# A two-layer encoder on one core: modulation columns by 32x32 transposes on VectorE, and GpSimd's branch ahead of its index wait

## What is computed

```python
for l in range(DEPTH):
    mod = ca @ w_ada[l] + b_ada[l]                    # (1, 6 * 1024)
    sh1, sc1, gt1, sh2, sc2, gt2 = split(mod, 6)
    h = rms_norm(x, g_norm1[l]) * (1.0 + sc1) + sh1
    proj = h @ w_in[l]                                # groups A, B, C, D
    ...
    mix = concat([ya, yb, yc, yd]) @ w_out[l]
    x = x + gt1 * mix
    h2 = rms_norm(x, g_norm2[l]) * (1.0 + sc2) + sh2
    x = x + gt2 * hier_moe(h2, ...)                   # 32 experts, top 2
return rms_norm(x, g_final)
```

## Time and profile before

| | us |
|---|---|
| three runs | 2034.39, 2034.10, 2145.37 |
| median | 2034.39 |
| the profiled execution | 2032.44 |
| its span, first to last instruction | 2030.6 |
| PE busy in it | 1684.3 (83%) |
| DVE busy | 581.1 (29%) |
| ACT busy | 509.1 (25%) |
| POOL busy | 225.0 (11%) |
| mean granted clock of TensorE | 0.896 |

### The profile page before, as it was taken

How to read it: one execution, slowest core, us unless ns; L and a number is a source line. 1 busy time by engine, 2 the same in 40 slices (tenths; PEclk the granted TensorE clock), 3 DMA queues, 4 the chain that set the end, 5 groups by cost and what they waited for, 6 DMA issues and landing times. The chain is left out here.

```text
span 2030.6 us, 22742 instructions
## 1 busy us (share of the span) xinstructions
PE 1684.3 (83%) x7696; PEld 843.4 (42%) x7696; DVE 581.1 (29%) x1259; ACT 509.1 (25%) x1109; POOL 225.0 (11%) x223
## 2 busy tenths in 40 slices
PE   4999987998878988788849999889688788888882
PEld 3456544455333333333325655444534333333331
DVE  1373344233111111111146515432311111112114
ACT  2101745322111111112131026461111111112112
POOL 2000012010111011111130002021101111111101
PEclk7999967988999989899969998689699899999896
DMA  9423433126999889999971324320378999999993
GB/s 337 148 83 124 143 124 102 52 116 261 409 399 402 338 336 398 396 399 418 375 243 62 105 95 151 125 102 21 124 294 353 394 403 402 403 416 401 389 406 138
DMA packets 91445, 527.49 MB, mean 260 GB/s; under 512 B 13936, under 2 KB 20176, under 8 KB 66800
## 3 DMA queue, kind: packets, MB, share of 16 engines
q1 hardware_dynamic: 72720, 489.43, 61.2%
q0 software_dynamic: 13104, 24.51, 3.9%
q10 hardware_dynamic: 5552, 12.65, 1.7%
HBM read 521.04 MB, written 23.86 MB: 268 GB/s over the span
## 5 line engine op out<-in xcount | busy, mean ns | idle before, releaser
L1090 PE MATMUL ps<-ring,arena 128*64 128x512 f32 x2928 | 703.5, 639 | 160.0 <-DMA ring<-in_w_exp_up 140.9
L1090 PEld LDWEIGHTS ps<-ring,arena 128*64 128x64 f32 x2928 | 254.6, 147 | 565.6 <-issue 562.0
L822 PE MATMUL ps<-ring,hT 128*128 128x512 f32 (+1 forms) x1024 | 363.7, 513 | 6.5 <-ACT tmp L1260 4.9
L822 PEld LDWEIGHTS ps<-ring,hT 128*128 128x128 f32 x1024 | 192.4, 190 | 164.2 <-issue 147.3
L576 DVE TENSOR_TENSOR arena<-ps,arena 64x512 f32<-64x512 f32 (+1 forms) x64 | 44.4, 693 | 688.3 <-ACT arena L1359 443.3
L1359 ACT ACTIVATE arena<-ps 128x512 f32<-128x512 f32 x64 | 38.2, 597 | 618.5 <-PE ps L1090 586.1
L782 POOL DMA_INDIRECT yexp_d<-arena,masks x64 | 59.3, 927 | 927.0 <-DVE arena L584 927.0
L1351 ACT ACTIVATE arena<-ps,modc 128x128 f32<-128x128 f32 x256 | 96.4, 457 | 51.7 <-PE ps L1078 51.0
L565 DVE TENSOR_SCALAR arena<-ps,modc 128x128 f32<-128x128 f32 x256 | 87.4, 403 | 44.3 <-PE ps L1078 42.4
L1078 PEld LDWEIGHTS ps<-cst,arena 128*128 128x128 f32 x512 | 64.6, 195 | 66.3 <-issue 66.1
L1511 DVE SCALAR_TENSOR_TENSOR probsT<-z,convw,probsT 128x512 f32<-128x512 f32 x120 | 89.9, 751 | 3.6
(11 more groups left out here) (182 smaller groups left out, 1351.3 us busy)
## 6 DMA issues: line engine op xcount, KB each, us to landing
ring<-in_w_exp_gate SPq DMA_DIRECT2D x64, 2048.0 KB, 14.7
ring<-in_w_exp_up SPq DMA_DIRECT2D x64, 2048.0 KB
ring<-in_w_exp_down SPq DMA_DIRECT2D x64, 2048.0 KB, 10.0
ring<-in_w_ada SPq DMA_DIRECT2D x24, 2048.0 KB, 9.4
ring<-in_w_in SPq DMA_DIRECT2D x8, 2048.0 KB, 19.4
ring<-in_w_out SPq DMA_DIRECT2D x4, 2048.0 KB
ring<-in_w_in SPq DMA_DIRECT2D x6, 1024.0 KB, 16.8
xn_d<-arena ACTq DMA_DIRECT2D x8, 512.0 KB, 2.6
```

The costliest lines, as they stand in the source:

```text
L822: last = pe.matmul(out, lhs(k), rhs(k), start=(k == 0), stop=(k == n - 1))
L1090: last = [pe.matmul(outs[c][HALF * c:HALF * c + HALF, :], lhs(k)[:, 0:HALF], rhs(c, k), start=(k == 0), stop=(k == n - 1), tile_position=( ...
```

## The change

Ten column units are done in another way: units 6 to 9 of both layers, in the attention loop, and units 2 and 3 of layer 1, behind the lists (`turned_columns`). The first six of the program and all gates stay as they are. For a turned unit ACT makes no copy. DVE transposes the bank in blocks of 32x32 to `tmp` (`ada_turned`, two instructions of 128x256), so that the 32 equal rows of a group become 32 equal columns. `mod` then takes one column of each block and makes two products, with a stationary 128x32 table `fold32` of four stacked identities, which adds the four groups up, and eight moving columns. Apart from that, POOL's wait for the index list moves from ahead of the branch into both of its arms.

```diff
@@ CONSTS
-          "cosA": TT * DIFF, ...
+          "fold32": 32, "cosA": TT * DIFF, ...
@@ program
+        def turned_columns(l, u):
+            return u // 2 % 3 != 2 and (u >= NORM1_UNITS or (l and u >= NORM1_UNITS // 2))
@@ route (DVE)
             for m, u in ADA_NEXT[l][:2]:
                 mod_out(m, u)
+            for n, (m, u) in enumerate(ADA_NEXT[l][2:]):
+                ada_turned(m, u, n)
             link(slot_lists((l, "more_lists"), NE, P))
@@ gpsimd
                 words = wide_words(pool, l)
-                pool.wait_ge(gidx_ready, l + 1)
                 def gather(e):
                     def body(w):
+                        if e == 0:
+                            pool.wait_ge(gidx_ready, l + 1)
                         if e >= 2:
@@ mod (PE)
                 p0 = HALF * (u % 2)
+                if turned_columns(l, u):
+                    picked = tmp[:, part, :].rearrange("p (h k r) -> p h k r", h=2, k=KD)
+                    for h in range(2):
+                        q0 = p0 + 32 * h
+                        last = pe.matmul(bank(key)[q0:q0 + 32, 0:KD], C["fold32"], picked[:, h, :, 0],
+                                         start=True, stop=True, tile_position=(0, q0))
+                    fills(last, key)
+                    return
                 for k in range(KD):
@@ scalar, attention loop
                         m, u = ADA_LATER[l][n]
+                    if n is not None and not turned_columns(m, u):
                         if n >= 2:
@@ scalar, behind the lists
-                for n, (m, u) in enumerate(ADA_NEXT[l][2:]):
-                    await_filled(act, (m, "mod", u - 2))
-                    ada_out(m, u, n)
@@ vector
+            def ada_turned(l, u, part):
+                key = (l, "ada", u)
+                await_filled(dve, key)
+                src = bank(key).rearrange("p (h r k) -> p h k r", h=2, k=KD)
+                dst = tmp[:, part, :].rearrange("p (h k r) -> p h k r", h=2, k=KD)
+                for h in range(2):
+                    last = dve.transpose(dst[:, h], src[:, h])
+                drains(last, key)
@@ vector, attention loop
                     if ada_at(l, i - 1) is not None:
                         mod_out(*ADA_LATER[l][ada_at(l, i - 1)])
+                    n = ada_at(l, i)
+                    if n is not None and turned_columns(*ADA_LATER[l][n]):
+                        await_filled(dve, (ADA_LATER[l][n - 2][0], "mod", ADA_LATER[l][n - 2][1]))
+                        ada_turned(*ADA_LATER[l][n], n % 2)
```

More of the change, by code:

```diff
@@ L437, in program, with route @@
         HE = NE // 2
-        def route(dve, link, mod_out, l):
+        def route(dve, link, ada_turned, mod_out, l):
             key = (l, "logits")
@@ L1663, in _ @@
                         normalise(l, 2, [t])
-                route(dve, link, mod_out, l)
+                route(dve, link, ada_turned, mod_out, l)
                 experts_dve(dve, l)
@@ L1710, in shape_constants @@
     out["eps"] = np.full((P, 1), EPS)
+    out["fold32"] = np.tile(np.eye(32), (4, 1))
     table = np.concatenate([out[k] for k in CONSTS], 1).astype(np.float32)
```

2 lines of the change are left out of this document (1 added, 1 removed).

## The result

Over 20 runs each, the changed kernel's median is 2020.44 us and that of the kernel before 2033.81 us; the ratio is 0.9942, with a 95% interval of 0.9926 to 0.9958, so 12 us or 0.6% faster (9 to 15 us by the interval). The median lies outside the forecast range (2026.5 to 2036.0): the direction was right and the gain nearly three times the 4.4 us predicted. The prediction took 2% for about what a measurement of this kernel can tell from no change; with 20 runs of each the interval is 0.16% either way. The profiled execution took 2023.97 us, with a span of 2022.1 us. (One run of 9063.53 us stands alone and is left out of the ratio.)

What follows compares the result with a forecast made beforehand. Expert stages were taken as bound by the weight stream, attention by a PE and DVE loop. Attention's 2.7 us plus the tail's 1.7 made 4.4 us, for a median of 2030.0 us, eight in ten between 2026.5 and 2036.

Steps and rivals of the forecast that it cites:

- What bounds the kernel: Expert stages: bound by the stream of weights, DMA engines 0.94 busy at 380 GB/s; attention: paced by a PE and DVE loop.
- One for one: Expert stages: whatever starts expert 0's gate and up products earlier shifts the whole stage by the same amount.
- Part 1: Attention: eight short products become two, so six `mod` steps each lose a 0.46 us delay; 2.7 us won.
- so the whole delay is won and no more: late next is the mix: Attention's `mod` steps: `mod` ends ahead of the mix, so each step wins its 0.46 us delay only.
- the first rival: Attention: the clock falls sooner and gives the gain back, up to 5.7 us lost, 2033 to 2038.5 us; chance 0.14.
- The sign I had named for it: Attention: a mean clock under 0.80 would mean the clock falls sooner; 0.82 and 0.83 were forecast.
- Part 2: Attention: DVE's two transposes per unit take 0.83 us a pair, hidden in its idle time; cost nothing.
- The slow-transposes rival: DVE's queue in eight `ada` steps: transposes above about 1.1 us each outweigh the gain, 2036.3 us and somewhat above; chance 0.06.
- Its ScalarE term: Attention: ScalarE loses a 0.60 us copy per unit; it isn't on the loop, so counted as nothing.
- Part 3: Behind layer 0's lists: shorter products leave DVE last, and first tokens and gate and up products start 1.7 us earlier.
- Part 4: GpSimd's gathers: 0.3 to 1.0 us of branching moves ahead of the wait; worth nothing, since nobody waits.
- The sum: Whole program: 2.7 us from attention and 1.7 from the tail, 4.4 us in all; forecast median 2030.0 us.

Runs made afterwards that it cites:

- g1: The changed kernel with extra 128x128 products in TensorE's attention pauses, those of the second mean in a bank free at once; 1999.63 us, 0.9853 of the kernel before.
- g3: The changed kernel with extra products both in attention's pauses and in those between attention and the first expert; 1993.34 us, 0.9812 of the kernel before.
- f1: The kernel before, with 11 products of 128x128 filling the pause ahead of group B's first mean; 2027.15 us, 0.9985 of the kernel before.
- f3: The changed kernel with extra products in group A's pauses and ahead of both means, the second mean's behind a wait for its bank; 2012.28 us, ratio 0.9901 to before.
- f4: The kernel before, ScalarE's copies kept, with one of eight short products per turned attention unit; attentions 141.2 and 137.8 us, whole not compared.
- e2: The kernel before with only the columns behind layer 0's lists turned, attention and GpSimd as before; 2023.66 us, 0.9962 of the kernel before.
- e4: The changed kernel, also making the eight short products of before ahead of the two new ones; 2028.11 us, 0.9984 of the kernel before.

## Why the prediction was wrong

**What bounds the kernel** was right as far as the runs can tell: the medians of g1 and g3 are at least as much shorter as their stages ahead of the experts (19.9 us for 16.3 in the traces, 26.2 for 23), and in layer 0's experts the DMA engines stay at 0.94 and 380 GB/s. "One for one" is closer than the experts' stages, which vary by 7 to 9 us, let one see.

**Part 1, the `mod` steps** was right step by step. Late turns of 0.46 us are gone and the turn is 0.06 us behind the mix (0.05 foretold). The two products take 0.24 us, under the 0.45 I had set as the lower end; since PE then waits for the mix anyway, it changes nothing. "Six steps by 0.46 give 2.7 us" is 2.7 us as the runs have it up to step 23 (1.2 and 1.5), but that agreement is partly luck: the `mod` steps won 3.4 us, and the clock took 0.7 back in other steps.

**The step that failed** is the one behind it, "so the whole delay is won and no more: late next is the mix". It carries the gain of a step to the end of attention as if each later step kept its length. What the later steps take depends on the granted clock, and 2.5 and 2.3 us a layer came from one fall of it that no longer came, at group B's pause of 2.0 us, and from the shorter stretch at half clock behind it. I had considered the clock, but as the first rival and with one sign only: it was to fall sooner, and give the gain back. It had a chance of 0.14 and a price of the right size (up to 5.7 us; measured 4.9), and the wrong direction. The sign I had named for it, a mean clock in attention under 0.80, couldn't show this: the mean went from 0.82 to 0.83, as forecast, and the gain lay inside it. The rule I weighed (the Trainium skill, TensorE: Matmul & The Clock Gate, "HAM oscillation — how this bites in real kernels": idle gaps on PE put its clock down) is borne out by f1, f3 and g1, where filled pauses keep the clock up. What I had not done is to look which pauses the falls of the trace followed: group B's of 2.0 us was in the timeline of before, with a half-clock stretch right behind it, and a row on it would have opened a case on the fast side.

**Part 2, the transposes** was right: 0.41 to 0.45 us each (mean 428 ns over 20 records), 0.78 a pair since the two overlap, against 0.83, and hidden. The slow-transposes rival is out. Its ScalarE term, nothing, stands too (f4: at most 0.2 us a layer).

**Part 3, the tail** was right in its mechanism: DVE last, 9.5 us from the end of the first lists to the first tokens (467.83 to 477.35; foretold 9.5). The first turn comes 1.8 us sooner and the gate and up products 1.9, for 1.7. But it ended at the start of gate and up, "the gate and up products then start ... and their loads follow", while the products themselves became 0.9 us shorter through the clock. The same failed step, a second time.

**Part 4, GpSimd** was right: the gather 1.06 us sooner (foretold 0.3 to 1.0), and nobody waits.

**The sum** would have been 2.7 + 4.9 + 1.9 + 0.9 = 10.4 us with the clock's two terms; the ratio says 9 to 15, so what is left is within its interval and needs no cause. **The range** was too narrow on the fast side: below the forecast it allowed 3.5 us, with two full-clock steps of 0.95 us for the clock, above it 6 us with a rival of its own, while the trace had six falls in each layer's attention and nothing that fixed their sign.

## What to carry to other kernels

Where the granted clock alternates, list its falls with the pause that each follows, and price any edit ahead of them with one stretch at half clock either way: in layer 0, 1.2 us less ahead of one pause brought 2.5 more, and 1.6 us of added work made the attention 4.1 us longer. Then ask whether the pauses themselves can go, which was worth twice the change under study: idle products into a bank that is about to be overwritten, as many as fit the pause and ahead of the wait, took 26 us more off the kernel. They must be issued where the bank is free already; behind the wait they cost their full time at half clock.

## What the hardware showed that I had not expected

- From 307 to 320 us of the changed kernel PE is busy 10.75 of 13.00 us at 1.2 GHz, and the clock does not rise; with its pauses filled, the same steps run at 2.4 GHz, for 86 us without a fall in f3.
- The clock's changes come at a few places behind a stage's first `ada` in kernel after kernel: where group A's pauses are not filled, the first rise in attention comes at 57.0 to 58 us or at 50.7 to 51.1, and the same kernel can show either.
- Of two pauses of 2.0 us, at the same place of layer 1's work, one was followed by a fall of the clock and one was not; they began 13.71 us (e2) and 13.57 us (e4) behind the clock's last rise.
- A DVE transpose of 128x256 f32 in 32x32 blocks, from PSUM with strided operands on both sides, takes 0.41 to 0.45 us, a pair 0.78; a product of 128x128 f32 0.235 us at full clock, a pair with 8 columns each 0.24.
- Equal kernels' attentions can differ by 3.4 us (141.0 and 137.5 in two traces of the changed kernel), and their projections too (164.8 or 168.1).
